# A two-layer hybrid trunk on one core: gate products in twos, half products' low parts moved, and the attention's value sums put behind the whole value projection

## The reference, cut to what matters

```python
def forgetting_attention(x, w_in, b_f, w_out):           # layer 0
    q, k, v, fg = split(x @ w_in)
    c = cumsum(log_sigmoid(fg + b_f))
    logits = q @ k.T / 8 + c_i - c_j                     # causal
    return (softmax(logits) @ v) @ w_out

def rglru_block(x, ...):                                 # layer 1
    xb, gb = split(x @ w_in)
    xb = causal_dwconv(xb, conv_w, conv_b)               # 4 taps
    r, ig = sigmoid(xh @ w_a + b_a), sigmoid(xh @ w_i + b_i)   # 8 blocks of 128
    # a = exp(-8 r softplus(-lam)); h = scan(a, sqrt(1 - a^2) * ig * xb)
    return (h * gelu(gb)) @ w_out

def conv_ffn(x, w_up, conv_w, conv_b, w_down):           # both layers
    val, gate = split(causal_dwconv(x @ w_up, conv_w, conv_b))   # 2 x 2816 channels
    return (gelu(gate) * val) @ w_down

x = layer_norm(ALPHA * x + mixer(x)); x = layer_norm(ALPHA * x + conv_ffn(x))
x = x + sigmoid(x @ gate_w + gate_b) * (p @ ple_w)
```

## Time and profile before

| what | us |
|---|---|
| median of three runs | 1230.15 (1229.83 to 1232.99) |
| profiled execution, its own time | 1228.31 |
| its span | 1226.3 |
| PE busy | 1218.3 (99%) |
| PEld busy | 1011.1 (82%) |
| DVE busy | 840.8 (69%) |
| POOL busy | 745.3 (61%) |
| ACT busy | 504.5 (41%) |

### The profile page before, as it was taken

How to read it: one execution, slowest core, us unless ns; L and a number is a source line. 1 busy time by engine, 2 the same in 40 slices (tenths; PEclk the granted TensorE clock), 3 DMA queues, 4 the chain that set the end, 5 groups by cost and what they waited for, 6 DMA issues and landing times.

```text
span 1226.3 us, 17972 instructions
## 1 busy us (share of the span) xinstructions
PE 1218.3 (99%) x6165; PEld 1011.1 (82%) x6165; DVE 840.8 (69%) x1172; ACT 504.5 (41%) x834; POOL 745.3 (61%) x846
## 2 busy tenths in 40 slices
PE   9999999999999999999999999999999999999998
PEld 6777777787898988888888778888889888888887
DVE  6555556588877747899753375289777757799742
ACT  4445444223444423664244385013344423564141
POOL 7554557809999897300377556938998998200273
PEclk9999999999999999999999999999999999999999
DMA  5221233302223243776153222311323234676121
GB/s 202 71 69 69 66 105 97 127 1 78 95 71 134 69 154 120 248 207 198 52 170 104 70 85 84 119 57 56 111 74 120 86 138 137 206 219 198 63 96 60
DMA packets 74203, 137.54 MB, mean 112 GB/s; under 512 B 4272, under 2 KB 52976, under 8 KB 73632
## 3 DMA queue, kind: packets, MB, share of 16 engines
q1 hardware_dynamic: 73088, 134.23, 33.5%
q10 hardware_dynamic: 1056, 2.58, 0.5%
HBM read 134.60 MB, written 2.20 MB: 112 GB/s over the span
## 4 chain that ended last, share of the span: by engine, by line
PE 95%; DVE 2%; ACT 1%; DMA 1%; DVEq 1%; issue 0%; ACTq 0%; SPq 0%
PE bank L622 16%; PE bank L624 16%; PE bank L623 16%; PE bank L1024 4%; PE bank L1026 4%; PE bank L1025 4%; PE bank L641 4%; PE bank L643 4%; PE bank L642 4%; PE bank L974 3%; PE bank L976 3%; PE bank L978 3%; PE bank L916 2%; PE bank L918 2%; PE bank L737 2%; PE bank L923 1%
## 5 line engine op out<-in xcount | busy, mean ns | idle before, releaser
L608 POOL TENSOR_TENSOR w_lo<-stage,w_hi 128x256 fp32r<-128x256 f32 x528 | 407.8, 803 | 28.5 <-DVE w_lo L1506 7.7
L600 POOL TENSOR_SCALAR w_hi<-stage 128x1024 fp32r<-128x1024 f32 x132 | 155.5, 1178 | 301.6 <-PE bank L643 166.2
L622 PE MATMUL bank<-x_hi,w_hi 128*128 128x512 f32 (+1 forms) x520 | 201.4, 387 | 1.4 <-DVEq L1430 1.4
L623 PE MATMUL bank<-x_lo,w_hi 128*128 128x512 f32 (+1 forms) x520 | 200.8, 386 | 0.0
L624 PE MATMUL bank<-x_hi,w_lo 128*128 128x512 f32 (+1 forms) x520 | 200.7, 386 | 0.0
L622 PE MATMUL bank<-in_hi,w_hi 128*128 128x512 f32 x312 | 130.0, 417 | 0.0
L1975 ACT ACTIVATE tmp<-bank,cols 128x512 f32<-128x512 f32 x88 | 63.7, 775 | 155.6 <-PE bank L624 119.5
L624 PE MATMUL bank<-in_hi,w_lo 128*128 128x512 f32 x312 | 122.1, 391 | 0.0
L623 PE MATMUL bank<-in_lo,w_hi 128*128 128x512 f32 x312 | 122.0, 391 | 0.0
L622 PEld LDWEIGHTS bank<-x_hi,w_hi 128*128 128x128 f32 x520 | 97.7, 188 | 21.3 <-DVEq L1430 2.2
L624 PEld LDWEIGHTS bank<-x_hi,w_lo 128*128 128x128 f32 x520 | 97.7, 188 | 19.8
(11 more groups left out here) (259 smaller groups left out, 2857.7 us busy)
## 6 DMA issues: line engine op xcount, KB each, us to landing
stage<-w_square SPq DMA_DIRECT2D x163, 512.0 KB, 3.4
stage<-w_down SPq DMA_DIRECT2D x52, 512.0 KB, 4.0
stage_far<-w_down SPq DMA_DIRECT2D x24, 512.0 KB, 4.6
rows<-norm_rows SPq DMA_DIRECT2D x4, 1024.0 KB, 5.7
outT<-x SPq DMA_DIRECT2D x7, 256.0 KB, 2.0
x<-xT SPq DMA_DIRECT2D x3, 512.0 KB, 6.8
p_in<-pT ACTq DMA_DIRECT2D x2, 512.0 KB, 5.2
w_ai<-w_lru SPq DMA_DIRECT2D x1, 1024.0 KB, 8.0
```

What stands on the lines that cost most here:

```text
L600: whole = pool.tensor_scalar(high[:, s, :], stage[:, s, :], 1.0, 0.0, ALU.mult, ALU.add)
L608: piece = pool.tensor_tensor(low[:, s, to], stage[:, s, to], high[:, s, to].bitcast(F32), ALU.subtract)
L622: pe.matmul(out, w_hi[:, s, c:c + P], m_hi, start=first, stop=False)
L623: pe.matmul(out, w_hi[:, s, c:c + P], m_lo, start=False, stop=False)
```

## The change

Four edits.

- Attention: `turn_values` moves from behind step 2 of the query projection to behind step 1 of the key projection, ahead of the first two turnings of head 0. The first turning of head 1 goes from step 0 to step 1 of the value projection. `sum_values` moves behind the whole value projection, directly ahead of the next scores. ACT copies the turned values behind the copies of turned head 0, and the new value projection (`values`) ahead of `outputs`. The last pair keeps its order.
- Recurrence: units of `rgx` 2 to 7 are made in twos, with the gate products of two blocks behind them.
- Feed-forward, both layers, on DVE: `half_low` of half 2 moves behind the first convolution and the sums of half 1, and the others move by one place.

```diff
-SECOND_AT = (0, 1, 5, 6, 6)
+SECOND_AT = (1, 1, 5, 6, 6)
@@ TensorE, loop over pairs
-                project(j, 0, 0, {TURN_AT: lambda: turn_values(j - 1)})
+                project(j, 0, 0)
                 scores(j - 1, 1)
-                project(j, 1, 1, head(j - 1, 0, FIRST_AT))
+                turns = head(j - 1, 0, FIRST_AT)
+                def values_and_probs():
+                    turn_values(j - 1)
+                    turns[FIRST_AT[0]]()
+                project(j, 1, 1, {**turns, FIRST_AT[0]: values_and_probs})
                 pe.wait_ge(exp_ready, j * 8 + 1)
-                project(j, 2, VALUE_BANK, head(j - 1, 1, SECOND_AT))
+                project(j, 2, VALUE_BANK, head(j - 1, 1, SECOND_AT, slice(0, 3)))
+                sum_values(j - 1, (0, 1))
+                sum_values(j - 1, (2, 3))
@@ TensorE, recurrence
-            for m in range(2, KT):
+            for m in range(2, KT, 2):
                 pe.wait_ge(rg_conv, m - 1)
-                rg_tile("rgx", m, m % 2)
+                rg_tile("rgx", m, 0)
+                pe.wait_ge(rg_conv, m)
+                rg_tile("rgx", m + 1, 1)
                 rg_gate_products(m - 2)
+                rg_gate_products(m - 1)
@@ VectorE, conv_ffn
                 half_sums(2)
-                half_low(layer, 2)
                 conv_half(layer, 0, 0)
                 half_sums(1)
-                half_low(layer, 0)
+                half_low(layer, 2)
                 conv_half(layer, 0, 1)
                 half_sums(3)
+                half_low(layer, 0)
+                conv_half(layer, 1, 0)
                 half_low(layer, 1)
-                conv_half(layer, 1, 0)
                 half_low(layer, 3)
@@ ScalarE, attend
                 exponentials(j, 0, not first)
-                token_values(j)
+                if not project_it:
+                    token_values(j)
                 exponentials(j, 1, not first)
                 turned_probs(j, 0, not first)
                 if project_it:
+                    token_values(j)
                     keys(j_next)
                 turned_probs(j, 1, not first)
-                outputs(j)
                 if project_it:
                     values(j_next, True)
+                outputs(j)
```

## The result

The changed kernel takes 1235.17 us (median of 8 runs, 1233.88 to 1237.19) against 1229.99 us (8 runs, 1229.17 to 1232.99): ratio 1.0042, 95% interval 1.0034 to 1.0051. It is 5.2 us slower; 1235.8 was forecast.

A forecast was written before the change was run, and what follows sets the result against it. PE, busy 99% of the span, bounds the kernel. Iterations 2 to 6 +5.3, 1 -0.15, 7 +1.1, behind the loop +0.5, feed-forward -0.98, recurrence -0.12: +5.65 on 1228.31, plus 1.84 to the median, gives 1235.8 us; range 1228.7 to 1238.8.

The forecast's parts named there:

- Mask at E + 2.31: Attention loop: DVE's mask for head 0 comes at E + 2.31 instead of E + 1.49, 0.82 us later.
- E: Start of the scores of head 0 in an attention iteration, from which all times of that iteration are counted.
- DVE's loop turn: Attention: DVE's sequencer is busy turning its loop, so `mixed` cannot slip and the mask shifts 0.82 us, not 0.14.
- Two blocks: Attention iterations 2 to 6: POOL's rounding and first subtraction each block a DVE scaling; +1.06 us an iteration, chance 0.50.
- joining the turnings: PE's own stream in the attention: fewer interruptions and a short stop gone, -0.09 us an iteration without new stops.
- Iteration 7: Attention loop's iteration 7: already blocked scalings end later, PE stops 1.65 us; about 25.9 us long, +1.1 us.
- Feed-forward: First DVE release in each layer: DVE's convolution starts 0.49 us earlier, and PE too; -0.98 us for two layers.
- Recurrence: Units and gate products in twos: three interruptions of 0.03 to 0.04 us go, -0.12 us.
- Behind the loop the same 0.82, less 0.13 of PE's, lengthens the stop of 0.8: PE's stop at the first output products behind the attention loop grows: +0.5 us, between 0.2 and 0.8.
- one block: Rival, attention: only POOL's rounding blocks a scaling, +0.48 us an iteration, +1.75 us in all, 1231.9 us; chance 0.23.
- no block: Rival, attention: head 1's mask stays in time or the loop's turn hides; -1.1 us, 1229.0 us; chance 0.18.
- the last pair's share: Stretch behind the attention loop until the last value sums, forecast +0.5 us.

The follow-up runs named there:

- The run with the mask first: Changed kernel with DVE making the next pair's head 0 masks and maxima ahead of `mixed`: 1228.31 us, ratio 0.9991 to the kernel before.
- The run with POOL held: Changed kernel with POOL starting the loop's query unit only when head 0's scaling is done, mask still late: 1228.87 us, ratio 1.0002 to the kernel before.
- the faster of the last two versions: Changed kernel with the mask ahead of `mixed` and the last pair's turned values behind step 5, not 2: 1227.07 us, ratio 0.9978 to the kernel before.
- the attention alone: Kernel before with only the attention's edits, feed-forward and recurrence as before: 1235.73 us, ratio 1.0052.
- the sums alone: Kernel before with only the sums moved behind the whole value projection and `values` ahead of `outputs`: 1232.95 us, ratio 1.0028.
- the feed-forward alone: Kernel before with only the feed-forward's edit, `half_low` moved: 1228.90 us, ratio 0.9997.

## Why the prediction was right, step by step

- **Mask at E + 2.31.** Measured 136.42 - 134.11 = 2.31. The reading of DVE's loop turn was right. The profile's own releaser was not wrong: in iteration 1 of before, with no `mixed` ahead, the scores alone held the mask until E + 1.50, so both limits lay together. The run with the mask first shows the scores' limit in the new order, E + 1.61.
- **Two blocks.** Scalings expected from 7.17 to 9.8, measured 7.16 to 9.79; mask of head 1 expected 9.99, measured 9.98; third turning 15.38 against 15.37; iteration 25.44 against 25.45. The run with POOL held shows that the block is the cause and not its companion. Two small terms of the sum were off and cancelled: joining the turnings gives 0.15 us an iteration and not 0.09 (24.24 with the mask first), and the 0.15 us at the scores of head 1, a second effect of the late mask, stood at nothing. With them PE reached the third turning at E + 14.34, not 14.24, and stopped 1.03 us, not 1.15.
- **Iteration 7.** 25.9 expected and measured.
- **Feed-forward.** -0.49 us a layer expected and measured at the stop itself.
- **Recurrence.** -0.12 expected, -0.26 in both profiles: 0.09 us an interruption and not 0.03 to 0.04, a mis-sized term, and small.
- **Wrong: "Behind the loop the same 0.82, less 0.13 of PE's, lengthens the stop of 0.8".** It became shorter, 0.57 us. I moved DVE by 0.82 and left POOL where it was. Two things were off. The mask of the last pair moved by 0.60 only, from E + 1.49 to E + 2.09, since on leaving the loop DVE is ready 0.38 us behind `mixed` and not 0.59. And the value projection now ends 2.3 us ahead of the scores, so POOL starts its unit 2.3 us earlier and, as it runs without a break there, its rounding is over as the scalings begin. Scalings of 2.79 us in place of 3.53 took back what the shift cost. In iterations 2 to 6 POOL waits for the query projection anyway and the earlier start doesn't matter.
- **Not in the forecast: 0.7 us before the first scores, 1.0 and 1.7 us in layer 0's feed-forward, 0.6 in layer 1.** They follow no edit. The 0.7 us are a wait for `fg` that only this profile and that of the faster of the last two versions have. The rest of layer 0's up projections changes by +1.0 us with the attention alone, +0.7 with the sums alone, 0.0 with the mask first; layer 0's down projection by 0.0 with the attention or the feed-forward alone, +0.9 with the sums alone, +1.3 with the mask first and with POOL held. Of the two listed stops in that projection, one stands behind sums of weights that DVE could start only when `stage<-w_down` had landed, the other behind a `w_lo` of DVE that took 2.91 us for 1.82 while a sum of POOL, begun at such a landing, ran beside it. I take them for what differs between executions, which spread over 3.3 us in the eight runs; what sets them was not tried and stays open.
- Of the rivals, "one block" is what the sums alone do, and "no block" is what POOL held back does. The forecast of the time, 1235.8 against 1235.2, owes a little to luck. The terms that it forecast came to 4.9 us for 5.65, the last pair's share being the largest miss (-0.1 for +0.5). The unforecast stretches add about 3.9 us between the two profiles, nearly what the profiles' distance exceeds that of the medians by (3.6 us). That they hardly weigh in the medians is an inference, as only one execution of each kernel was profiled.

## What to carry to other kernels

When a step is moved on the engine that bounds the kernel, follow the last instruction of each other engine's loop body: what it waits for also holds the top of the next iteration, and a releaser named by the profile may only be the later of two that lie together. Then lay the moved instructions over the other engine that shares their ports: a shift of 0.8 us that nearly fits the slack by itself cost 1.1 us an iteration because it ended under a 1 us instruction. Before giving up an order that loses, look for the instruction that delays the chain and needn't be ahead of it: here one DVE step placed behind the next maxima turned +0.42% into -0.09%, at the edge of its interval, and with the last pair's turned values moved as well into -0.22%.

## What the runs showed of the hardware that I had not expected

- Who comes first decides, within 0.3 us. POOL's rounding at E + 7.46 blocked the third scaling of the changed kernel, shown from E + 7.63. In its iteration 7 and with the sums alone the scaling that was blocked is shown starting 0.03 us ahead of the rounding and together with it. With the scalings 0.7 us earlier the last one started 0.3 us ahead of the rounding; there the rounding lost 0.06 us and the scalings none (1.27 us).
- The Trainium skill, "SBUF — State Buffer", section "Who interferes with whom", says that the one who issues second fully blocks until the first finishes. The trace agrees for one instruction against one. Between two streams the ports changed hands after each instruction: 2.63 us of four scalings held one rounding and one subtraction, and POOL's rounding was only 0.12 us longer.
- The turn of DVE's hardware loop, from the end of `mixed` to the first mask of the next iteration, took 0.59 to 0.60 us in iterations 3 to 7 of all four kernels in which the sums were moved and `mixed` stayed last, where the profile shows nothing to wait for. The first turn took 0.63 us and the way out of the loop 0.38.
